# A pair of operand tiles put at the same byte modulo 512 as the streamed weights

## What is computed

```python
# experts of the first block (per token: 8 heads x 16 chosen experts)
act = gelu(einsum("td,thkd->thk", xb, expert_down[idx]))
y   = einsum("thk,thkd->td", gate * act, expert_up[idx])
# feed-forward of the second block
u = causal_dwconv(h @ w_up, conv_w, conv_b)
x = x + (gelu(u) * (h @ w_gate)) @ w_down
# embedding under a gate
x = x + (p @ w_ple) * sigmoid(rmsnorm(x, ple_norm) @ w_ple_gate)
```

## Time and profile before

| what | before |
|---|---|
| time, median of 3 runs | 1327.23 us (1326.96 to 1327.52) |
| profiled execution: time | 1327.35 us |
| profiled execution: span, first to last instruction | 1325.5 us |
| TensorE busy | 1307.9 us, 99% |
| TensorE weight loads busy | 1178.0 us, 89% |
| VectorE, ScalarE, POOL busy | 957.1 us (72%), 737.1 us (56%), 518.4 us (39%) |
| granted TensorE clock, mean | 0.998 |
| matmuls `ps<-whi,phi`, `ps<-wlo,phi`, `ps<-whi,plo` | 600 of each, 512 columns |
| matmuls with `parts` stationary | 136 of each |

### The profile page before, as it was taken

How to read it: one execution, slowest core, us unless ns; L and a number is a source line. 1 busy time by engine, 2 the same in 40 slices (tenths; PEclk the granted TensorE clock), 3 DMA queues, 4 the chain that set the end, 5 groups by cost and what they waited for, 6 DMA issues and landing times. The chain is left out here.

```text
span 1325.5 us, 25837 instructions
## 1 busy us (share of the span) xinstructions
PE 1307.9 (99%) x8501; PEld 1178.0 (89%) x8501; DVE 957.1 (72%) x1810; ACT 737.1 (56%) x1121; POOL 518.4 (39%) x276
## 2 busy tenths in 40 slices
PE   9999999999999999999999999999999999999997
PEld 8999899999999999998888888888889888888886
DVE  6885677999898467775666666666667668777775
ACT  6833557777777643334444444444465457555556
POOL 1010002888887888787788788100000000000000
PEclk9999999999999999999999999999999999999999
DMA  7459554767777766667778777777664335555551
GB/s 258 148 193 384 192 182 147 187 179 186 178 187 177 191 173 150 151 143 207 213 213 209 208 210 213 256 233 229 217 243 160 116 108 180 190 187 191 191 190 64
DMA packets 119324, 253.00 MB, mean 191 GB/s; under 512 B 44336, under 2 KB 60848, under 8 KB 118752
## 3 DMA queue, kind: packets, MB, share of 16 engines
q1 hardware_dynamic: 77232, 229.24, 53.3%
q0 software_dynamic: 42032, 22.99, 10.9%
HBM read 234.23 MB, written 17.96 MB: 190 GB/s over the span
## 5 line engine op out<-in xcount | busy, mean ns | idle before, releaser
L459 DVE TENSOR_TENSOR wlo<-raw,whi 128x1024 fp32r<-128x1024 f32 x412 | 503.2, 1223 | 133.0 <-ACT whi L446 122.4
L412 POOL DMA_INDIRECT gates_dense<-gate,spot x256 | 506.9, 1980 | 166.9 <-issue 78.1
L446 ACT ACTIVATE whi<-raw 128x1024 fp32r<-128x1024 f32 x412 | 434.7, 1057 | 239.6 <-PE ps L465 227.6
L463 PE MATMUL ps<-parts,whi 128*128 128x256 f32 x1472 | 422.7, 287 | 2.2 <-DVE parts L550 2.0
L464 PE MATMUL ps<-parts,whi 128*128 128x256 f32 x1472 | 416.4, 283 | 0.0
L465 PE MATMUL ps<-parts,wlo 128*128 128x256 f32 x1472 | 416.2, 283 | 0.0
L463 PEld LDWEIGHTS ps<-parts,whi 128*128 128x128 f32 x1472 | 282.6, 192 | 5.5 <-issue 4.2
L464 PEld LDWEIGHTS ps<-parts,whi 128*128 128x128 f32 x1472 | 282.1, 192 | 0.0
L465 PEld LDWEIGHTS ps<-parts,wlo 128*128 128x128 f32 x1472 | 282.0, 192 | 0.0
L463 PE MATMUL ps<-whi,phi 128*128 128x512 f32 x600 | 238.1, 397 | 2.0 <-DVE plo L1874 1.4
L464 PE MATMUL ps<-wlo,phi 128*128 128x512 f32 x600 | 237.9, 396 | 0.0
(11 more groups left out here) (374 smaller groups left out, 1273.5 us busy)
## 6 DMA issues: line engine op xcount, KB each, us to landing
raw<-in_wts SPq DMA_DIRECT2D x412, 512.0 KB
gates_dense<-pf POOLq DMA_DIRECT2D x4, 4096.0 KB, 30.9
gd<-gates_dense SPq DMA_DIRECT2D x22, 256.0 KB, 4.5
gd<-gates_dense SPq DMA_DIRECT2D x10, 512.0 KB, 5.7
gates_dense<-gate,spot POOLq DMA_INDIRECT x256
cst<-in_c POOLq DMA_DIRECT2D x1, 1216.0 KB, 6.4
xt<-in_x_tok SPq DMA_DIRECT2D x2, 512.0 KB, 4.4
kk<-in_keys POOLq DMA_DIRECT2D x1, 1024.0 KB, 5.4
```

Of the source, the lines that this page charges most:

```text
L412: pl.indirect_dma_start(out=dense, out_offset=bass.IndirectOffsetOnAxis(ap=spot[:, tb, h, k:k + 1], axis=0), in_=gate[:, tb, h, k:k + 1], ...
L446: nc.scalar.activation(whi[:, j, :], raw_tile(j // 2, j % 2), ACT.Copy).then_inc(s["w_hi"], 1)
L459: nc.vector.tensor_tensor(wlo[:, j, :], raw_tile(j // 2, j % 2), whi[:, j, :].bitcast(F32), ALU.subtract).then_inc(s["w_lo"], 1)
L463: nc.tensor.matmul(out_ap, wh, xh, start=first, stop=False, skip_group_check=True)
```

## The change

`phi` and `plo` are placed directly behind `parts`, with an assertion that they begin at the same byte modulo 512 as `whi`. `vec`, `warm` and `wm` become one tensor `words` of 832 bytes (`warm` has seven words and not eight, so a dummy activation writes another word). The tiles `oh2` and `oheq` of the gates' stage, which lie over the pair, move with it. The arena, and `xt` and `pf` before it, begin 32 bytes lower modulo 512. In the second block a gap is put before `pthi`, so that it and `ptlo` also begin at the remainder of `whi`. No instruction is added, removed or moved on any engine.

```diff
@@ def program
         raw = place("raw", [2, 2 * TW])
+        whi_at = top[0]
         whi = place("whi", [RING, TW], F32R)
         wlo = place("wlo", [RING, TW], F32R)
         parts = place("parts", [2, KT, T], F32R)
         ahi, alo = parts[:, 0, :, :], parts[:, 1, :, :]
+        pairs = top[0]
+        assert pairs % 512 == whi_at % 512, pairs
+        phi = place("phi", [2, T], F32R)
+        plo = place("plo", [2, T], F32R)
+        pairs_end = top[0]
         ident = place("ident", [P])
         ones = place("ones", [P])
-        vec = place("vec", [N_CV])
-        warm = place("warm", [8])
-        wm = place("wm", [KT])
+        words = place("words", [N_CV + KT + 7])
+        vec, wm, warm = words[:, 0:N_CV], words[:, N_CV:N_CV + KT], words[:, N_CV + KT:]
         eps = warm[:, 6:7]
         small = top[0]
+        assert small % LINE == 0, small
         xt = place("xt", [TB, D])
         pf = place("pf", [2, T])
         aux_end = top[0]
-        phi = place("phi", [2, T], F32R)
-        plo = place("plo", [2, T], F32R)
...
-        aux = [aux_end]
+        aux = [pairs]
         oh2 = place("oh2", [2, P, GT], F16, at=aux)
         oheq = place("oheq", [2, SPLIT, GT], F16, at=aux)
-        assert aux[0] <= top[0]
+        assert aux[0] <= pairs_end
...
         pt = place("pt", [2, T], at=a)
+        a[0] += (whi_at - a[0]) % 512
         pthi = place("pthi", [2, T], F32R, at=a)
         ptlo = place("ptlo", [2, T], F32R, at=a)
...
-            A(warm[:, 7:8], ones[:, 0:1], ACT.Sqrt)
+            A(warm[:, 1:2], ones[:, 0:1], ACT.Sqrt)
```

More of the change, by code:

```diff
@@ L36 @@
 EPS = 1e-6
+LINE = 64
 MH, MD = 8, 64
@@ L167, in program @@
         arena = top[0]
+        assert arena % LINE == 0, arena
         ea = place("ea", [N_EXP, T])
@@ L322, in _ @@
             sp.dma_start(xt[:, 1, :], x_tok[:, 1, :]).then_inc(s["x_in1"], 16)
-            sp.dma_start(vec[:, :], vecs).then_inc(s["vec_in"], 16)
+            sp.dma_start(vec, vecs).then_inc(s["vec_in"], 16)
             rs = (s["raw0"], s["raw1"], s["raw2"], s["raw3"])
```

## The result

The changed kernel takes 1330.92 us (median of 8 runs, 1329.06 to 1332.15), the kernel before in the same rounds 1327.1 us: ratio 1.0028, 95% interval 1.0019 to 1.0037. That is 0.28% slower, just over the 0.2% that can be told from no change, and 16.7 us above the 1314.2 forecast.

A forecast was written before the change was run, and what follows sets the result against it. TensorE was taken to bound the kernel, by the start-to-start distance of its matmuls in the experts' up-projection. 11.7 + 1.3 + 0.1 = 13.1 us off the profiled 1327.35 gave 1314.2 us; 8-in-10 range 1310 to 1325.

The forecast's parts named there:

- (a): Experts' up-projection: `phi` and `plo` at `whi`'s remainder shorten 1536 matmul steps from 234.3 to 226.7 ns, 11.7 us.
- half: Rival, 10%: an equal remainder is not enough, 3.2 ns lost a matmul; gain 8.0 us, 1319.3, range 1318 to 1324.
- nothing: Rival, 10%: remainder innocent, the 7.6 ns have another cause, first of all rewriting of the operand; 1327 us.
- a worse lock: Rival, 5%: new offset makes weight load's reads meet the stream's worse; steps of 0.24 us, 10.4 us more, 1338.
- (b): Feed-forward: the same address gain on 22 tiles of 12 matmuls, each down to 2.75 us, 1.3 us in all.
- (c): Embedding: 24 matmuls from 234 to 229 ns, 0.1 us.
- (d) to (f): VectorE and ScalarE at other bytes, arena shifted 32 bytes, one tensor for three: nothing, (e) bounded at 1 us either way.
- The step that failed: POOL's gate scatters before tile 88: 60 of 83 shorten with the tile, 5.5 us; SyncE's net wait 2.8 us, cost 0.
- the room: Gates of tile 88: load done by 842.8, first use 847.66, 4.9 us, plus 3 us by which the multiplication leads.
- Slower: scatters miss their gap: Rival, 3%: VectorE's gap before `plo` shrinks by 0.09, a missing scatter waits a tile, 2.7 us; 14 missed give 1344.

The follow-up runs named there:

- without the deadline: Changed kernel, SyncE not waiting for the second half's scatters, tiles 88 to 127 without that half's gates: 1315.17 us; same in the kernel before: 1326.65 us.
- the exchange of the multiply: Changed kernel with VectorE's multiplication by the gates issued behind `plo` and not ahead of it, everything computed: 1331.24 us.
- a cut of `wlo`: Changed kernel, experts' second layer `wlo` in two instructions: 512 and 512 columns 1315.1 us, 896 and 128 1315.28 us, 768 and 256 1315.06 us.
- kernels at 32 and 64: Changed kernel, pair 32 or 64 bytes past `whi`'s remainder, second half's gates of tiles 88 to 127 left out, no scatter wait: 1324.05 and 1325.85 us.

## Why the prediction was wrong

**(a) right.** "1536 x (234.3 - 226.7) ns = 11.7 us, all on the path": the step is 226.7 ns, and without the deadline the stage goes from 361.50 to 349.96 us, 11.5 less. The rivals of half and nothing and that of a worse lock are out. The Trainium skill ("TensorE: Matmul & The Clock Gate", Step-by-step: what each phase is for) has the weight load take no read bandwidth from the stream; by that no address would matter, and the trace does not agree: only the pair and the few small tiles beside it moved, and the step with them, from 226.7 ns to 233.3. Whether it is the weight load that meets the stream, no run shows.

**(b) too large.** 1.3 us were forecast for the feed-forward. From 1106.02 to 1285.72 us before and from 1108.15 to 1287.51 after, between the same matmuls, lie 179.70 and 179.36: 0.34 us. Its down tiles did become shorter, 2.58 to 2.51 us from the first to the last of twelve (228.4 ns a step), 1.4 us for the 21 in this stretch, as forecast. But the wide tiles, for which the sum has no term, became longer. Of the 20 stretches between two down tiles every second took 5.78 us before and the others 5.88; after, all take 5.87. With 0.15 us ahead of the first down tile 1.0 us went back. Why a stretch takes one or the other, no run shows. (c) was right to the 0.1 us; (d) to (f) show nothing: with (a) and (b) the kernel without the deadline should come to 1327.35 - 11.5 - 0.3 - 0.1 = 1315.4, and came to 1315.16.

**The step that failed** is that on the scatters: "the scatters are tied to the tiles ... At that share some 60 of the 83 since 605 us will shorten with the tile, 5.5 us in all", and from it "Net wait: 1.0 + 1.8 = 2.8 us" and "I take 0". The 60 did shorten, 2.81 to 2.72 us. What I left out are the others, three in eight tiles at 1.85 to 1.93 us, which I took for free of the tile and thus unchanged. They exist only because of a coincidence of less than 0.1 us. A held scatter starts (duration of `wlo` + 1.42 + 0.30 - tile) behind the next `wlo`: 1.22 + 1.72 - 2.81 = 0.13 us before, 1.22 + 1.72 - 2.72 = 0.22 after. Once in eight tiles VectorE's loop comes round and `wlo` is 0.12 us late; that leaves 0.01 before (quick, and two more with it) and 0.10 after (held). Released 6.5 us later where the sum had 5.5 earlier, SyncE waited 14.9 us and not 2.8. The row that could have told it was in the prediction: the scatter of 829.79 that ends at 832.30, "already after VectorE has begun again". I read it as proof that a scatter doesn't need the pause; it is a held one.

A second term failed with it: the room. "Room is 4.9 + 3" counts from the load of the gates, and by it a wait of 14.9 us would have cost 7.0 us. But the weights stand behind the same wait, and of them only 2.6 us were in flight, so 12.3 were lost, and 1.5 more at the lower clock, for which the prediction has no term.

**The rival "Slower: scatters miss their gap"** was right in place and in sign: SyncE's wait, weights queued behind it, PE dry near tile 88. Its mechanism was not: no gap became too short, as the exchange of the multiply shows. Its scale (14 missed, 1344) was too high, since a scatter that loses its quick turn loses 0.87 us and not a tile. I gave it 3 in 100, because I judged the scatters by their share of one-a-tile steps and did not ask what the three others hung on.

## What to carry to other kernels

Try the stationary and the moving operand of float32r matmuls at the same byte modulo 512: 7.6 ns of 234 here, 11.5 us in all, and it takes a cut of `wlo` (1315.1 to 1315.3 us, the fastest that compute everything) to see it in the time. When an engine gets faster, list the queues with a deadline against it and, for each, the rows that are quicker than their kind; ask what lets them be quick and by how much it would be missed. A long VectorE instruction beside indirect DMAs on POOL is worth cutting in two where somebody waits for the DMAs and VectorE isn't the bound, even at 14.8 us more of VectorE's time; where nobody waits it gives nothing (1327.24 us in the kernel before).

## What the runs showed of the hardware

- The distance from one 512-column float32r matmul to the next depends on where the stationary pair lies in SBUF. By its bytes past the moving operand modulo 512: 226.7 ns at 0, 233.3 at 32, 64 and 320, 234.3 at 352. The moving operand's own place was never changed.
- An indirect DMA on POOL that starts while a VectorE subtraction or multiplication with two SBUF inputs is running ends 1.42 us behind that instruction's end, for lengths of 0.28 to 1.22 us. The edge for the 1024-column subtraction lies between 0.03 and 0.04 us behind its start: up to 0.03 the DMA takes 1.54 us and slows the subtraction from 1.22 us to between 1.26 and 1.28, at 0.04 it takes 2.61 (kernels at 32 and 64). Between 640 and 830 us all 7 starts at 0.01 to 0.03 were quick and all 48 at 0.12 to 0.16 held before, and all 47 at 0.10 and 0.22 held after. The Trainium skill ("SBUF — State Buffer", Who interferes with whom) says that such an instruction contends with one of GpSimd that reads SBUF and that the order of issue decides who blocks. The trace agrees for the indirect DMA that starts second: it is held. It does not for VectorE: `wlo` at 722.83, in the middle of the scatter from 721.99 to 723.53, takes its usual 1.22 us. The same section infers that the generation of descriptors is not touched by a `tensor_tensor`; here the indirect DMA was. Which part of a scatter is held, and why for 1.42 us past the end, no run shows.
- After 12.3 us without a matmul the granted clock was 0.50, 1.2 GHz, and seven steps took 1.5 us more.
- Waits that are already fulfilled cost a scatter on POOL nothing that can be seen: 0.30 us between two with none and with five.
